# Mixture-of-experts block: experts visited in an order of rank, scatter weights turned at an expert's head, the seventh tile of down rows loaded in one transfer, TensorE's bodies on nested else

## The reference, cut to what matters

```python
N_EXPERTS = 8; TOP_K_EXPERTS = 2; D_FF_EXPERT = 3584
logits = h @ w_router                       # h: 256 x 1024
top_val, top_idx = lax.top_k(logits, 2)     # each token goes to two of eight experts
gate = jax.nn.softmax(top_val, axis=-1)
...
def _swiglu(h, wg, wu, wd):
    return (jax.nn.silu(h @ wg) * (h @ wu)) @ wd
# y[token] += gate * _swiglu(rows of the expert, w_gate[e], w_up[e], w_down[e])
```

## Time and profile before

| | us |
|---|---|
| median of 3 runs | 1768.75 (1766.95 to 1779.86) |
| profiled execution, its own time | 1774.51 |
| its span | 1772.7 |
| PE busy in the span | 1594.6 (90%) |
| DMA queue q1, share of 16 engines over the span | 74.3% |

### The profile page before, as it was taken

How to read it: one execution, slowest core, us unless ns; L and a number is a source line. 1 busy time by engine, 2 the same in 40 slices (tenths; PEclk the granted TensorE clock), 3 DMA queues, 4 the chain that set the end, 5 groups by cost and what they waited for, 6 DMA issues and landing times.

```text
span 1772.7 us, 19682 instructions
## 1 busy us (share of the span) xinstructions
PE 1594.6 (90%) x8282; PEld 872.2 (49%) x8283; DVE 409.1 (23%) x867; ACT 226.2 (13%) x439; POOL 0.2 (0%) x4
## 2 busy tenths in 40 slices
PE   5999889999989998797597999999999998999975
PEld 5778658777658784432132333334444433333321
DVE  4265523323333633400101002002000110100103
ACT  1122210000011321110011011111011001111101
POOL 0000000000000000000000000000000000000000
PEclk9999899999989998799799999999999999999998
DMA  9955525665745440099999999897666599999995
GB/s 348 326 203 177 190 95 190 237 237 190 262 136 181 167 181 19 3 378 371 342 389 371 382 378 370 327 389 279 248 248 235 208 327 388 370 389 371 389 371 217
DMA packets 168108, 482.18 MB, mean 272 GB/s; under 512 B 10472, under 2 KB 20992, under 8 KB 167936
## 3 DMA queue, kind: packets, MB, share of 16 engines
q1 hardware_dynamic: 168064, 481.57, 74.3%
HBM read 480.49 MB, written 1.05 MB: 272 GB/s over the span
## 4 chain that ended last, share of the span: by engine, by line
PE 74%; SPq 8%; DVE 8%; DMA 6%; issue 3%; ACT 2%; DVEq 0%; ACTq 0%
PE bank L830 14%; PE bank L879 10%; PE bank L640 7%; SPq L527 6%; PE bank L841 6%; PE bank L777 6%; PE bank L826 6%; PE bank L791 4%; DMA ring<-in_w_exp_down 4%; DVE acc L1004 4%; PE bank L759 3%; PE bank L873 3%; PE bank L634 2%; PE bank L962 2%; SPq L533 1%
## 5 line engine op out<-in xcount | busy, mean ns | idle before, releaser
L830 PE MATMUL bank<-ring,hT 128*64 128x448 f32 x1792 | 353.8, 545 | 45.6 <-issue 19.3
L879 PE MATMUL bank<-ring,bt 128*32 128x256 f32 (+1 forms) x1680 | 239.9, 495 | 24.5 <-DMA ring<-in_w_exp_down 12.3
L830 PEld LDWEIGHTS bank<-ring,hT 128*64 128x64 f32 x1792 | 130.0, 137 | 265.9 <-issue 205.9
L1342 DVE TENSOR_TENSOR bt<-bt,bank 128x448 f32<-128x448 f32 (+1 forms) x52 | 32.4, 622 | 807.6 <-PE bank L830 555.0
L879 PEld LDWEIGHTS bank<-ring,bt 128*32 128x32 f32 (+1 forms) x1680 | 86.0, 125 | 160.5 <-issue 119.1
L777 PE MATMUL bank<-hT,ring 128*128 128x256 f32 x704 | 156.0, 383 | 1.2 <-DVE hT L1075 1.2
L640 PE MATMUL bank<-hT,ring 128*128 128x256 f32 x640 | 152.9, 396 | 2.3 <-ACT hT L1424 1.2
L777 PEld LDWEIGHTS bank<-hT,ring 128*128 128x128 f32 x704 | 134.6, 192 | 21.7 <-issue 1.9
L640 PEld LDWEIGHTS bank<-hT,ring 128*128 128x128 f32 x640 | 124.4, 198 | 23.4 <-DVE hT L1075 3.1
L1004 DVE SCALAR_TENSOR_TENSOR acc<-ring,cond,acc 128x512 f32<-128x512 f32 x160 | 120.3, 752 | 5.6
L841 PE MATMUL bank<-ring,hT 128*32 128x448 f32 x1024 | 102.9, 542 | 0.0
(11 more groups left out here) (204 smaller groups left out, 999.8 us busy)
## 6 DMA issues: line engine op xcount, KB each, us to landing
ring<-in_w_exp_gate SPq DMA_DIRECT2D x128, 896.0 KB, 10.4
ring<-in_w_exp_up SPq DMA_DIRECT2D x128, 896.0 KB, 15.1
ring<-in_w_exp_down SPq DMA_DIRECT2D x64, 1536.0 KB, 16.3
ring<-in_w_ada SPq DMA_DIRECT2D x24, 2048.0 KB, 10.4
ring<-in_w_in SPq DMA_DIRECT2D x10, 2048.0 KB, 11.1
ring<-in_w_exp_down SPq DMA_DIRECT2D x64, 256.0 KB, 16.8
ring<-in_w_ff_gate SPq DMA_DIRECT2D x5, 2048.0 KB, 18.6
ring<-in_w_ff_up SPq DMA_DIRECT2D x5, 2048.0 KB, 14.0
```

The source lines that it names most:

```text
L830: last = mm(o[64 * c2:64 * c2 + 64, 0:EH], xsT[:, k, t0:t0 + 64], w[:, k, c2 * EH:(c2 + 1) * EH], start=(k == 0), stop=(k == KC - 1))
L879: last = mm(bank[4 + 2 * u][m * c:m * c + m, 0:D // parts], hsT[:, u, at_:at_ + m], ed[:, t, c * (D // parts):(c + 1) * (D // parts)], sta ...
```

## The change

- **Order.** DVE sorts the experts behind the router: a key of 16 times the class less the expert's number, with 80 added for expert 0 so that it stays first, is sorted by `max` and `max_index`, and `TURNS` puts rank 0, 1, 7, 2, 6, 3, 5, 4 at turns 0 to 7. Row 0 of `route_i` now holds the expert's number for each turn, row 1 the class for each turn, row 2 the first token by expert. SP and DVE read the expert's number at run time; SP's weight addresses are now dynamic, but for expert 0.
- **Scatter weights.** PE turns `selg` into bank 1 at the head of an expert, ACT copies it to `selgT`, and `hidden` waits for that (`sgt_a`) ahead of its first write to bank 1. At the end, ACT copies column half 0 of the output and DVE half 1; PE multiplies half 0 into banks 2 and 3 as soon as ACT is done, half 1 into banks 6 and 7 as soon as DVE is done. The wait for `yzero_v` moves forward in a step, ahead of the first use of bank 2 or 3. DVE makes the next scatter weights before the last output copies, not behind the clearing.
- **Seventh tile.** One transfer of 512 KB to 128 partitions for two of 256 KB to 64 partitions.
- **Bodies.** PE's four bodies hang on nested else, and the loop's first instruction is put at slot 0 of an instruction block.

```diff
+TURNS = (0, 1, 7, 2, 6, 3, 5, 4)
...
+        def expert_of(eng, r, last=NE - 1):
+            return eng.value_load(route_i[0:1, 0, bass.ds(r, 1)], min_val=0, max_val=last)
+
+        def start_of(eng, e):
+            return eng.value_load(route_i[0:1, 2, bass.ds(e, 1)], min_val=0, max_val=2 * T)
...
             for J in range(NE * ES):
-                e, j0 = J // ES, J % ES * EW
+                r, j0 = J // ES, J % ES * EW
+                if J == 0:
+                    e = 0
+                elif J % ES == 0:
+                    if r == 1:
+                        sp.wait_ge(route_v, 1)
+                    e = expert_of(sp, r)
+
+                def rows_of(w, lo, n, a, b):
+                    return w[0, bass.ds(e, 1), lo:lo + n, a:b].rearrange("e r n -> (e r) n")
...
                 room(J, TAIL - D, TAIL, d_used, 3 * J)
-                for i in range(2):
-                    r0 = j0 + i * EH + 3 * P
-                    sp.dma_start(ed[64 * i:64 * i + 64, 6, :], w_exp_down[0, e, r0:r0 + 64, :]).then_inc(full_d[2], 16)
+                last = rows_of(w_exp_down, j0, EW, 0, D).rearrange("(i r) n -> i r n", i=2)[:, 3 * P:EH, :]
+                sp.dma_start(ed[:, 6, :], last).then_inc(full_d[2], 16)
...
+                    if i == 0 and a == 1 and k == 0:
+                        pe.wait_ge(sgt_a, r + 1)
...
-                    pe.wait_ge(yzero_v, r + 1)
+                    pe.wait_ge(yzero_v, r + 1)
...
-                for b in range(2):
-                    for hf in range(2):
+                for hf in range(2):
+                    pe.wait_ge((ys_a, ys_v)[hf], r + 1)
+                    for b in range(2):
                         for q in tiles:
-                            last = mm(bank[4 + 2 * b + hf][:, :], selgT[:, q, b * P:(b + 1) * P],
+                            last = mm(bank[(2, 6)[hf] + b][:, :], selgT[:, q, b * P:(b + 1) * P],
...
+            with nc.Fori(0, NE, engines=PE, head_slot={PE[0]: 0}) as r:
+                pe.wait_ge(xsT_v, r + 1)
                 which = class_of(pe, r)
-                pe.wait_ge(xsT_v, r + 1)
-                for n in range(1, 5):
-                    with pe.If(which == n):
-                        with pe.Fori(0, ES) as s:
-                            step(r, r * ES + s, n)
-                        scatter(r, n)
+                with pe.If(which == 1):
+                    expert(r, 1)
+                with pe.Else():
+                    with pe.If(which == 2):
+                        expert(r, 2)
+                    with pe.Else():
+                        with pe.If(which == 3):
+                            expert(r, 3)
+                        with pe.Else():
+                            expert(r, 4)
...
-            signal(nc.vector.tensor_copy(route[:, 0, 0:NE], starts), dv)
-            then(nc.vector.tensor_copy(route[:, 1, 0:NE], total))
+            then(stt(rank[:, 0, :], total, float(2 * NE), ct[:, C_IOTA:C_IOTA + NE], ALU.mult, ALU.subtract))
+            then(ts(rank[:, 0, 0:1], rank[:, 0, 0:1], float(10 * NE), None, ALU.add))
+            then(nc.vector.max(rank[:, 1, :], rank[:, 0, :]))
+            then(nc.vector.max_index(topi[:, 0, :], rank[:, 1, :], rank[:, 0, :]))
...
+            for to, fro in enumerate(TURNS):
+                signal(nc.vector.tensor_copy(route[:, 0:2, to:to + 1], rank[:, :, fro:fro + 1]), dv)
```

More of the change, by code:

```diff
@@ L816, in _, with hidden @@
                 last.then_inc(gat_p, 1)
-            def hidden(J, n, i, a, unit, c=0):
+            def hidden(r, J, n, i, a, unit, c=0):
                 kind, t0 = unit
@@ L910, in step @@
                 elif n == 3:
-                    hidden(J, n, 0, 0, A, 0)
-                    hidden(J, n, 0, 1, A, 0)
+                    hidden(r, J, n, 0, 0, A, 0)
+                    hidden(r, J, n, 0, 1, A, 0)
                     pe.wait_ge(esg_a, 4 * J + done(n, 0))
-                    hidden(J, n, 1, 0, A, 1)
+                    hidden(r, J, n, 1, 0, A, 1)
+                    pe.wait_ge(yzero_v, r + 1)
                     turn_hidden(J, n, 0, "wide", bank[3], 0)
-                    hidden(J, n, 1, 1, A, 1)
+                    hidden(r, J, n, 1, 1, A, 1)
                     quarter(B[1], range(0, 6))
@@ L966, in _, with expert @@
             pe.wait_ge(route_v, 1)
-            with pe.Fori(0, NE) as r:
-                which = class_of(pe, r)
-                pe.wait_ge(xsT_v, r + 1)
-                for n in range(1, 5):
-                    with pe.If(which == n):
-                        with pe.Fori(0, ES) as s:
-                            step(r, r * ES + s, n)
-                        scatter(r, n)
+            def expert(r, n):
+                scatter_matrix(r, n)
+                with pe.Fori(0, ES) as s:
+                    step(r, r * ES + s, n)
+                scatter(r, n)
+            PE = (mybir.EngineType.PE,)
+            with nc.Fori(0, NE, engines=PE, head_slot={PE[0]: 0}) as r:
+                pe.wait_ge(xsT_v, r + 1)
+                which = class_of(pe, r)
+                with pe.If(which == 1):
[8 more added lines that the diff above has]
+                            expert(r, 4)
         @block.vector
@@ L1347, in expert_end @@
                 window(r + 1)
[L1348 to L1352, removed]
+                scatter_weights(r + 1)
+                ve.wait_ge(d_used, 3 * ES * r + 3 * ES)
+                if n < 3:
+                    last = nc.vector.tensor_copy(ys[0:64, 0, CW:D], bank[4][64:P, :])
+                else:
+                    last = nc.vector.tensor_copy(ys[:, 0, CW:D], bank[5][:, :])
                 if n in (2, 3):
                     s0, q = (64, 0) if n == 2 else (0, 1)
-                    for c in range(4):
+                    for c in (2, 3):
                         last = nc.vector.tensor_copy(ys[s0:s0 + 32, q, c * T:(c + 1) * T],
@@ L1358, in expert_end @@
                 elif n == 4:
-                    for hf in range(2):
-                        last = nc.vector.tensor_copy(ys[:, 1, hf * CW:(hf + 1) * CW], bank[6 + hf][:, :])
+                    last = nc.vector.tensor_copy(ys[:, 1, CW:D], bank[7][:, :])
                 last.then_inc(ys_v, 1)
@@ L1550, in step, with scatter_matrix @@
                     turned_hidden(J, n, 3, 1, 1, bank[3])
+            def scatter_matrix(r, n):
+                tiles = 2 if n > 2 else 1
+                ae.wait_ge(sgt_p, r + 1)
+                act(selgT[:, 0:tiles, :].rearrange("p q n -> p (q n)"), bank[1][:, 0:tiles * T], ACT.Copy).then_inc(sgt_a, 1)
             def expert_end(r, n):
                 ae.wait_ge(d_used, 3 * ES * r + 3 * ES)
[L1555 to L1559, removed]
+                if n < 3:
+                    ins = act(ys[0:64, 0, 0:CW], bank[4][0:64, :], ACT.Copy)
+                else:
+                    ins = act(ys[:, 0, 0:CW], bank[4][:, :], ACT.Copy)
+                if n in (2, 3):
+                    s0, q = (64, 0) if n == 2 else (0, 1)
+                    for c in (0, 1):
+                        ins = act(ys[s0:s0 + 32, q, c * T:(c + 1) * T], bank[6][32 * c:32 * c + 32, 0:T], ACT.Copy)
+                elif n == 4:
+                    ins = act(ys[:, 1, 0:CW], bank[6][:, :], ACT.Copy)
                 ins.then_inc(ys_a, 1)
```

80 lines of the change are left out of this document (44 added, 36 removed).

## The result

The changed kernel takes 2069.31 us (2065.6 to 2072.6), the kernel before beside it 1774.3: a ratio of 1.1662, 95% interval 1.1596 to 1.1727. It is 295 us slower where 34 less were forecast. Nearly all of the loss is in one edit, the seventh tile of down rows in one transfer, and that transfer is slow for a reason that no row of before could show. In what follows the short fall of the DMA rate of the earlier trace rows is called a dip, the long and deep one of the changed kernel a trough.

A forecast was written before the change was run, and what follows sets the result against it. DMA was taken to bound class-1 experts, PE classes 2 and 3. Experts, gap and branches summed to 974.3 us against 1008.3, so 34.0 saved: 1768.75 - 34.0 = 1735 us, range 1715 to 1760.

The forecast's parts named there:

- If it runs like the other 128-partition pieces, the dip goes: Merged seventh-tile load: a DMA step falls from 29.06 to 27.05 to 27.3 us; at worst all the dip stays.
- expert 0 with the gap: First expert 93.2 us without dips, plus 21.9 for PE's code-fetch gap and the slow clock after it.
- expert 7: Class-1 expert after class 3: four DMA steps, 108.4 us, less DMA's largest lead of 17.0, so 91.4.
- experts 5 and 1: Class-1 experts visited after class 2: DMA's lead of 16.4 us gives 92.0; 94 each taken, 188 together.
- Gap of PE: PE jumping over unfetched bodies after expert 0: 19.3 us kept, 21.9 with the slow clock, before the class-3 expert.
- Rival (a): Shorter code fetch after expert 0 through nested else: 7 of 19.3 us stay, 1720 us in all; chance 0.17.
- Rival (d): PE's code fetched at each change of body, seven times 19.3 us: 1826 us in all; chance 0.05.
- Ends and heads: At each expert's end, scatter products start 1.6 us after the down product; 0.7 us gained in classes 2 and 3.
- the turning at the first head: New wait for the scatter weights (sgt_a), 6 us into an expert's first step behind one ACT copy: costs nothing.
- Order: Each class-1 expert but the first follows one that lets DMA run ahead, by 17.0 us at most.
- Addresses: SP's register arithmetic for loads: 2 to 5 us of 27 a step, covered by queued transfers, so nothing.
- Rival (c): The merged transfer still dips: experts sum to 1015.8 us, 7.5 more than before, 1776 us in all; chance 0.08.

The follow-up runs named there:

- turned_in_dve: Changed kernel, seventh tile one transfer of 128 rows contiguous in memory, DVE writing the second half's hidden columns tail first: 1741.31 us, ratio 0.9776.
- turned_chain: turned_in_dve with PE's four bodies on separate ifs as before the change, and the loop's head where it falls: 1746.65 us.
- before_one: The kernel before with only the seventh tile's merged transfer, source [2][64][1024]: 2058.91 us, ratio 1.1596.
- after_two: Changed kernel with the seventh tile loaded by two transfers again, all else kept: 1786.92 us, ratio 1.0061.
- turned_number: turned_in_dve with the experts visited in the order of their numbers: 1744.58 us, ratio 0.9832.
- before_turned: The kernel before with only the contiguous seventh tile in one transfer, hidden columns turned by DVE: 1745.59 us, ratio 0.9806.
- after_contig: Changed kernel with the seventh tile as one transfer of 128 contiguous rows, hidden columns turned tail first by added PE matmuls: 1766.6 us, ratio 0.9946.
- turned_first: turned_in_dve with the first expert's scatter weights made ahead of the clearing of four banks: 1734.72 us, ratio 0.9778.

## Why the prediction was wrong

**The step that failed** is "If it runs like the other 128-partition pieces, the dip goes", with its bound "at worst all of it stays". The merged transfer doesn't run like them: it costs some 11 us a step where 2 were to be gained. The rows of before held pieces whose outermost dimension is 128 or 64 only, so they said nothing of 2; I took "128 partitions" for what makes a piece fast, and left the term no bound on the side of a loss. The Trainium skill (DMA: Bandwidth & Descriptors, "Why a DMA increments its semaphore by 16 and not by 1") says that the number of engines is the largest up to 16 that divides the slowest dimension of both sides; for `[2][64][1024]` that is 2. The trace agrees: 47 to 55 GB/s, where two times 25.4 is 51. It was the rule to look for, and I weighed another page instead.

**The same term, when the transfer is made right,** was sound: no dip in the DMA-bound experts, and turned_in_dve takes 1741.31 us against a point of 1735 (the kernel before beside it stood at 1779.67). Its terms, forecast and measured: expert 0 with the gap 115.1 and 107.1; class 3, 204.4 and 206.3; expert 7, 91.4 and 94.8; the three of class 2, 374.4 and 367.8; experts 5 and 1, 188 and 198.4; with 1 for branches in the forecast, in all 974.3 and 974.4, counted from a head that comes 2.8 us later than before. That the sums agree is luck: the terms are off by 2 to 10 us and cancel.

**Gap of PE.** Forecast at 19.3 and the slow clock behind it, measured 10.5, and 5.84 in the changed kernel. Rival (a), with 7, was nearer, but its 1720 us did not come; turned_chain shows nested else and the slot together as the cause. That code is fetched in the gap was read from a queue's packets and stays a reading. Two numbers fit it: five packets with the chain of ifs and two with nested else, and a shorter gap for the same way of branching where the weight stream has troughs (12.81 us in before_one against 19.28; 5.84 in the changed kernel against 10.51 in after_two). Rival (d) fell: in turned_in_dve the chain shows one more gap, of 1.1 us. By number (turned_number) two of 4.3 and 4.4 us take the place of the 10.5, and both stand where an expert follows one of the same class; the one other there is 1.2 us.

**Ends and heads.** In class 2 of turned_in_dve the last down product ends at 1277.9 and the next expert's first starts at 1283.2:

```profile
1273.71 4.19 PE L899 MATMUL bank<-ring,bt 128*64 128x512 f32 x60
1279.38 3.70 PE L984 MATMUL bank<-arena 128*128 128x512 f32 x8 [1.48 <-ACT arena L1622]
1282.91 0.38 PE L973 MATMUL bank<-ct,arena 128*128 128x128 f32 x2
1283.23 0.97 PE L849 MATMUL bank<-ring,hT 128*64 128x448 f32 x4
```

That is 5.3 us for the 8.0 of the earlier trace rows: 2.7 gained, forecast 0.7. The start of the scatter products was forecast well (1.48 for 1.6); what was left out is that the eight products themselves then take 3.70 us for 5.40. What the forecast priced at nothing, the turning at the first head, costs: in the changed kernel PE waits 4.92 us for DVE's scatter weights behind the clearing of four banks, where it waited 2.67 for the tokens.

```profile
749.03 0.52 PE L973 MATMUL bank<-ct,arena 128*128 128x128 f32 x2 [4.92 <-DVE arena L1364]
```

With the same wait turned_in_dve stands there at 752.37, so this wait does not explain that its head is later.

**Order.** Credited with the leads of three class-1 experts (7, 5 and 1); worth some 5 us on the flat stream and nothing that can be told with dips. With dips a pair of classes 1 and 2 needs 232.4 us of DMA in any order, and PE's 213 (88 and 125) fit inside; only a lead after class 3 counts, and both orders have one. After class 2 on the flat stream class 1 took 98.8 and 99.6, not 94.

**Addresses** cost nothing that can be told, as forecast. The ranks are computed in every run made from the changed kernel, by number too, so no run prices the added DVE instructions.

**Rival (c)**, the dip stays, was the nearest to what happened and stopped far short of it (1776 us): it had a transfer no better than two, never one worse.

## What to carry to other kernels

Before two transfers are merged, write down the shape of both sides as the instruction will carry it, and look at the outermost number: here it, not the partitions reached, set the rate. Of 2, 4, 16 and 128 only 128 on both sides gave the flat stream; if the rows don't lie together, change which rows make the tile (here by having DVE, which has time to spare, write the hidden columns in another order) rather than leave a gap in the source. And when a term rests on "like the others", ask what the others have in common that this one lacks; if no row shows it, the price needs a bound on the bad side too.

## What the runs showed of the hardware that was not expected

- A 512 KB load whose source is `[2][64]` rows of 4096 bytes brings the stream down to 47 to 55 GB/s for some six us, with 10% to 20% of the DMA engines busy, one of `[4][32]` to 96 to 120; with one of `[128]` rows the stream stays at 407. In a stream of 11.01 MB a step the first costs some 11 us a step in classes 1 and 2 (40.0 to 40.3 us a step against 29.1).
- With `[16][8]` rows the trough is gone and a dip to 172 to 279 GB/s of some six us stays; a class-1 step takes 30.3 us where the flat rate needs 27.05. Its cause is open.
- In after_two the dip of the half-partition transfers is longer than in the earlier trace rows, 243 to 273 GB/s for five slices of 1.5 us:

```profile
GB/s 262 243 251 264 272 382 406 411 401 409 406 401 416 401 404 409 414 409 410 410 245 247 245 273 262 387 399 418 389 413 413 397 413 399 413 403 413 411 401 410
```

  That profiled execution took 1798.21 us, near the top of its spread. In its other steps the rate is below 370 GB/s for four to seven slices; by number, with dynamic addresses or constant ones, for three to five. So the length goes with the order of the experts, in one profile of each; why, no run shows.
- Turning the same columns by six small float32 products, each with one half of the identity, takes about three times as long as by three transposes: 12 instructions in 1.55 us, against three in 0.55.
- PE's gap behind expert 0 is 19.2 to 19.6 us with a chain of ifs (before, before_turned, turned_chain) and 10.3 to 10.5 with nested else at slot 0 in rank order, where the stream has no troughs (after_two, after_contig, turned_in_dve, turned_first).
